# Stick-breaking attention: cumulative products from rounded high and low parts of L

## The reference

```python
z = einsum('bqhd,bkhd->bhqk', q, k) * scale
log_1m = where(mask, log_sigmoid(-z), 0.0)
rest = cumsum(log_1m, axis=3, reverse=True) - log_1m
a = where(mask, exp(log_sigmoid(z) + rest), 0.0)
out = einsum('bhqk,bkhd->bqhd', a, v)
```

## Time and profile before

| | us |
|---|---|
| median of three runs (2595.11 to 2599.73) | 2596.3 |
| the profiled execution | 2597.36 |
| its span | 2595.4 |
| PE busy | 2520.1 (97%) |
| DVE busy | 1105.5 (43%) |
| ACT busy | 851.9 (33%) |
| POOL busy | 918.0 (35%) |

### The profile page before, as it was taken

One profiled execution on the slowest core, in us unless ns is written; L12 is line 12 of the kernel. 1 busy time (PEld: TensorE's weight loads), 2 busy tenths in 40 slices (PEclk: granted clock), 3 DMA queues, 4 the chain that ended last, 5 costly groups with the idle time before them and its releaser, 6 DMA issues.

```text
span 2595.4 us, 40399 instructions
## 1 busy us (share of the span) xinstructions
PE 2520.1 (97%) x16578; PEld 2205.8 (85%) x16578; DVE 1105.5 (43%) x1722; ACT 851.9 (33%) x1257; POOL 918.0 (35%) x382
## 2 busy tenths in 40 slices
PE   7999997999999999999999999999889999999999
PEld 6888887999999998777999999876566888888887
DVE  3883435365352522222562525434456433622222
ACT  3323322332222334544331222443335333422222
POOL 3221123244444441111354444431223454544443
PEclk9999999999999999999999999999999999999999
DMA  4110112132222221110222222321111322322222
GB/s 160 66 66 34 51 49 90 41 107 97 81 95 84 97 98 54 37 46 17 82 97 98 82 96 81 108 74 49 65 60 55 114 101 94 114 97 94 87 95 97
DMA packets 34002, 208.31 MB, mean 80 GB/s; under 512 B 3771, under 2 KB 7125, under 8 KB 9817
## 3 DMA queue, kind: packets, MB, share of 16 engines
q1 hardware_dynamic: 29552, 202.00, 22.0%
q10 hardware_dynamic: 4328, 4.54, 0.6%
HBM read 204.40 MB, written 2.12 MB: 80 GB/s over the span
## 4 chain that ended last, share of the span: by engine, by line
issue 62%; POOL 22%; PE 15%; POOLq 0%; DMA 0%; ACT 0%; ACTq 0%; DVE 0%; DVEq 0%
POOL wl L2397 22%; PE ps L365 13%; PE ps L318 1%; PE ps L302 1%; DMA arena<-in_extra 0%; POOLq L2396 0%; POOLq L2401 0%; DMA scratch<-arena 0%; PE ps L735 0%; ACT Hh L481 0%; ACT arena L486 0%; ACTq L700 0%; ACT wh L403 0%; PE ps L461 0%; ACTq L701 0%
## 5 line engine op out<-in xcount | busy, mean ns | idle before, releaser
L2397 POOL TENSOR_TENSOR wl<-raw,wh 128x1024 fp32r<-128x1024 f32 x376 | 917.7, 2444 | 1660.9 <-ACT wh L403 1660.9
L403 ACT ACTIVATE wh<-raw 128x1024 fp32r<-128x1024 f32 x376 | 395.1, 1054 | 844.2 <-PE ps L365 519.1
L365 PE MATMUL ps<-Hl,wh 128*128 128x264 f32 (+1 forms) x1896 | 489.7, 317 | 0.0
L365 PE MATMUL ps<-Hh,wl 128*128 128x264 f32 (+1 forms) x1896 | 488.0, 316 | 0.0
L365 PE MATMUL ps<-Hh,wh 128*128 128x264 f32 (+1 forms) x1896 | 487.1, 315 | 0.0
L365 PEld LDWEIGHTS ps<-Hh,wh 128*128 128x128 f32 x1896 | 312.3, 188 | 24.2
L365 PEld LDWEIGHTS ps<-Hl,wh 128*128 128x128 f32 x1896 | 311.6, 188 | 23.5
L365 PEld LDWEIGHTS ps<-Hh,wl 128*128 128x128 f32 x1896 | 311.7, 188 | 22.8
L318 PE MATMUL ps<-Hh,wh 128*128 128x264 f32 (+1 forms) x1056 | 287.1, 336 | 7.0 <-DVE arena L337 6.7
L318 PE MATMUL ps<-Hl,wh 128*128 128x264 f32 (+1 forms) x1056 | 261.3, 312 | 0.0
L318 PE MATMUL ps<-Hh,wl 128*128 128x264 f32 (+1 forms) x1056 | 260.9, 311 | 0.0
(11 more groups left out here) (259 smaller groups left out, 2982.0 us busy)
## 6 DMA issues: line engine op xcount, KB each, us to landing
raw<-in_w_all SPq DMA_DIRECT2D x188, 1024.0 KB, 4.7
X<-in_xT SPq DMA_DIRECT2D x4, 528.0 KB, 9.5
arena<-scratch ACTq DMA_DIRECT2D x2, 1024.0 KB
arena<-in_extra ACTq DMA_DIRECT2D x2, 528.0 KB
out<-X SPq DMA_DIRECT2D x1, 1024.0 KB, 4.2
out<-X SPq DMA_DIRECT2D x4, 256.0 KB, 2.0
arena<-in_extra ACTq DMA_DIRECT2D x2, 264.0 KB
cst<-in_consts SPq DMA_DIRECT2D x1, 448.0 KB, 11.3
```

The source lines that it names most:

```text
L365: mm = pe.matmul(ps[:, 2 * j + h + bank, 0:c1 - c0], w[:, j, k, :], x[:, blk, c0:c1], start=(at == 0 and part == 0), stop=(at == len(ks) - ...
L403: act.activation(wh[:, j], raw[:, j // 2, :, P * (j % 2):P * (j % 2) + P], ACT.Copy).then_inc(hi_split, 1)
L2397: pool.tensor_tensor(wl[:, j], raw[:, j // 2, :, P * (j % 2):P * (j % 2) + P], wh[:, j].bitcast(F32), ALU.subtract).then_inc(split_ready[j ...
```

## The change

L is written twice: as Lh, rounded to fp32r, and as Ll, what rounding left (also fp32r). The triangle and the square are rounded copies made once by ACT. `stick_cum` gets a `part`, 0 for the high and 1 for the low, and goes for every key tile over all later tiles itself; the sums of tiles on DVE and their semaphore `l_sums` are gone. PE's round is now: high products of step n-1, half of the fill (two groups), low products, the other half, value product, logits, with no exception for the fourth round. DVE computes max(z, 0) + E into Lh, again in f32 into E, and subtracts the one from the other into Ll (semaphore `l_low`). Because steps 2 and 3 of one pair no longer wait for the sums, the columns of tiles 2 to 4 have two places in L, used in turn (`l_turn`). The tables land at another place in the arena.

```diff
-        def stick_cum(pe, d, m):
+        def stick_cum(pe, d, m, part):
...
-            pe.wait_ge(sig["l_made"].sem, m + 1)
-            if x in (1, 2):
-                pe.wait_ge(sig["l_sums"].sem, 2 * b + x)
+            pe.wait_ge(sig["l_low" if part else "l_made"].sem, m + 1)
             for hh in range(2):
                 for s, c0, c1, at in STEP_PARTS[x]:
                     R = KEYTILE[s][1]
...
-                    mm = add("ntri", s, c0)
-                    for s2 in ((s + 1, s + 2) if x == 0 else (s + 1,)):
-                        if s2 <= 4 and max(c0, P * s2) < c1:
-                            mm = add("nones", s2, max(c0, P * s2))
-            sig["cum"].by(mm)
+                    for s2 in range(s, 5):
+                        lo = max(c0, P * s2)
+                        if lo < c1:
+                            rows, a = KEYTILE[s2][1], L_AT[s2] + l_turn(s2, b) - P * s2
+                            tri = d["ntri_r" if s2 == s else "nones_r"]
+                            mm = pe.matmul(ps[0:R, bank + hh, at + lo - c0:at + c1 - c0], tri[0:rows, 0:R],
+                                           d["L"][part][0:rows, hh, a + lo:a + c1], start=False, stop=True,
+                                           skip_group_check=True)
+            if part:
+                sig["cum"].by(mm)
...
             for n in range(STEPS + 2):
-                late = n % 4 == 3
-                if late:
-                    stick_fill(pe, n)
-                if 0 <= n - 1 < STEPS:
-                    stick_cum(pe, d, n - 1)
-                if not late:
-                    stick_fill(pe, n)
+                for part in range(2):
+                    if 0 <= n - 1 < STEPS:
+                        stick_cum(pe, d, n - 1, part)
+                    stick_fill(pe, n, part)
...
             act.activation(d["ident_r"], ident, ACT.Copy)
+            act.activation(d["ntri_r"], d["ntri"], ACT.Copy)
+            act.activation(d["nones_r"], d["nones"], ACT.Copy)
...
                     if n >= 2:
-                        act.wait_ge(sig["l_made"].sem, n - 1)
+                        act.wait_ge(sig["l_low"].sem, n - 1)
...
-                    sig["l_made"].by(v.scalar_tensor_tensor(
-                        out=L[:, :, STEP_L[x]:STEP_L[x] + w], in0=ps[:, bank:bank + 2, 0:w], scalar=0.0,
-                        in1=d["E"][:, n % 2, :, 0:w], op0=ALU.max, op1=ALU.add))
+                    dve.by(v.scalar_tensor_tensor(out=hi, in0=z, scalar=0.0, in1=e, op0=ALU.max, op1=ALU.add))
+                    dve.last(v)
+                    sig["l_made"].by(v.scalar_tensor_tensor(out=e, in0=z, scalar=0.0, in1=e, op0=ALU.max, op1=ALU.add))
+                    sig["l_made"].last(v)
+                    sig["l_low"].by(v.tensor_tensor(lo, e, hi.bitcast(F32), ALU.subtract))
```

More of the change, by code:

```diff
@@ L237, in program @@
             "g_conv", "g_silu", "prod_hi", "cv_tmp", "cv_hi", "cv_lo", "idx", "idx_relu", "idx_added", "z_made",
[L238 to L245, removed]
+            "z_log", "e_made", "l_made", "mask_ready", "cum", "a_exp", "oT_hi", "oT_lo", "rot_made", "rot_done",
+            "ret_s", "ret_a", "ret_o", "ret_var", "ret_std", "hn_sq", "hn_sum", "hn_std", "hn_done", "v_made",
+            "v_copied", "tb_made", "tb_copied", "tb_lo", "idx_dup", "idx_dup_read", "p_scores", "p_lo", "p_logits",
+            "p_exp", "p_diag", "p_turned", "p_copied", "p_av", "p_hi", "row_log", "row_scan", "bc_made", "bc_copied",
+            "m_w", "m_wd", "m_s", "m_a", "m_o", "m_ss", "m_std", "mg_sum", "mg_hi", "memset_done", "stage_dve",
+            "o_used", "row_done", "gain_both", "rs_first", "rs_mean", "rs_second", "gate_act", "row_bias", "out_gate",
+            "u_made", "u_read", "mo_exp", "m_sq", "e_read", "m_h", "m_hi", "m_y", "m_lo", "ret_center", "ret_t",
+            "ret_sum", "ret_sq", "ret_hi", "ret_y", "ret_lo", "l_low")}
         turn_done = [signal(f"turn_done{q}") for q in range(2)]
@@ L1486, in stick_views @@
             at = cut.at
-            L, E, A = cut(2 * TRI, h=2), cut(4 * 432, a=2, h=2), cut(4 * 432, a=2, h=2)
+            E, A = cut(4 * 432, a=2, h=2), cut(4 * 432, a=2, h=2)
             vT = Cut(at)(8 * T1, b=8)
[L1489 to L1492, removed]
+            cut = Cut(cut.at, arena_r)
+            Lh, Ll = cut(2 * TRI_2, h=2), cut(2 * TRI_2, h=2)
+            mask_r, ident_r, ntri_r, nones_r = cut(288), cut(P), cut(P), cut(P)
+            w = Cut(KB * T1 + at)
+            mask, ntri, nones = w(288), w(P), w(P)
+            return dict(V=V, E=E, A=A, vT=vT, mask=mask, ntri=ntri, nones=nones, L=(Lh, Ll), mask_r=mask_r,
+                        ident_r=ident_r, ntri_r=ntri_r, nones_r=nones_r)
+        TRI_2 = TRI + 432
         PAIRS = 8
@@ L1500, in program, with l_turn @@
         L_AT = [832, 432, 160, 16, 0]
+        def l_turn(s, b):
+            return TRI if s >= 2 and b % 2 else 0
         STEP_MASK = [(0, 288), (160, 288), None, (160, 288)]
@@ L1590, in stick_av, with stick_fill @@
             sig["o_used"].by(mm)
-        def stick_fill(pe, n):
+        def stick_fill(pe, n, part):
             b, x = n // 4, n % 4
             if b + 1 < PAIRS:
-                for k in range(4 * (x % 2), 4 * (x % 2) + 4):
-                    stick_group(pe, 2 * (b + 1) + x // 2, k)
+                k = 4 * (x % 2) + 2 * part
+                stick_group(pe, 2 * (b + 1) + x // 2, k)
+                stick_group(pe, 2 * (b + 1) + x // 2, k + 1)
             elif n < STEPS:
-                for k in range(2 * x, min(2 * x + 2, KB - 1)):
-                    out_group(pe, 0, k)
+                if 2 * x + part < KB - 1:
+                    out_group(pe, 0, 2 * x + part)
             elif n == STEPS:
-                pe.wait_ge(sig["a_exp"].sem, STEPS - 1)
-                for k in range(KB - 1):
+                if part == 0:
+                    pe.wait_ge(sig["a_exp"].sem, STEPS - 1)
+                for k in (range(4, KB - 1) if part else range(4)):
                     out_group(pe, 1, k)
@@ L1689, in stick_dve @@
             d = stick_views()
-            L = d["L"]
             evac_units(v, PLAN["c_v"], T1, d["vT"])
@@ L1695, in stick_dve @@
             for n in range(STEPS + 2):
[L1696 to L1706, removed]
-                if n < STEPS:
-                    x = n % 4
-                    w, bank = STEP_COLS[x], Z_BANK[n % 2]
+                if n < STEPS:
+                    b, x = n // 4, n % 4
+                    w, bank, a = STEP_COLS[x], Z_BANK[n % 2], STEP_L[x]
+                    if x == 0:
+                        a += l_turn(2, b)
+                    z, e = ps[:, bank:bank + 2, 0:w], d["E"][:, n % 2, :, 0:w]
+                    hi, lo = (part[:, :, a:a + w] for part in d["L"])
                     v.wait_ge(sig["z_log"].sem, n + 1)
```

## The result

The changed kernel takes 2641.55 us (median of four runs, 2641.08 to 2649.16), the kernel before 2596.02 (four runs): ratio 1.018, 95% interval 1.0159 to 1.020. It is slower by 45.5 us; the prediction said 2622.2 (+25.9) and a range up to 2634. The profiled executions took 2641.1 and 2597.4 us.

A forecast was written before the change was run, and what follows sets the result against it. TensorE was taken to bound the kernel, busy 97% at 2.4 GHz. Terms 25.0+1.1+0.3-0.9+0.4 gave +25.9 us on the profiled 2597.4, so 2623.3, and 2622.2 for the median; range 2604 to 2634.

The forecast's parts named there:

- The bound: Whole kernel: TensorE busy 97% of the span at 2.4 GHz, so a microsecond of matmul work is one of kernel.
- The products: Cumulative products at L1564's successor: 576 records against 384, 13.27 us per pair against 10.14, 25.0 us more in eight pairs.
- 16x16 product: Step 0's cumulative products: one rounded pass of the 16x16 matmul was priced at 0.125 us.
- the f32 break: Where a matmul's number of rows changes: drain 0.095 us and open weight load 0.107 us, taken to hold for fp32r too.
- Rival 1: 16-row products of steps 0 to 2: loads of rounded matmuls stay hidden through changes of rows; 2586 us, 10%.
- The vector side and the waits: Stick-breaking stage: VectorE's added work hides; waits add 1.1 and 0.3, logits save 0.9, the unit's evacuation adds 0.4 us.
- Rival 2: Stage's 32 steps: waits pile up, ACT late by 0.5 us in each, +16 us, 2638 us; 4%.
- The step that failed: Clock during cumulative products: 24 short matmuls at 1060 to 1064 stay at full clock, taken as evidence against rival 3.
- rival 3: Stick-breaking stage: breaks let the granted clock fall to 1.2 GHz over 20 us, costing as much again; 2642 us, 3%.

The follow-up runs named there:

- after_rows128: Changed kernel, but products with the last key tile (16 keys) take and write 128 rows, so no changes of rows: 2596.7 us, ratio 1.0002.
- before_later: Kernel before, with 20 matmuls issued twice at the end of the second FFN, a delay ahead of the last block: 2603.0 us, ratio 1.0032.
- rounded_sums: Changed kernel with 128 rows for the last key tile and running sums back on VectorE, split into high and low parts: 2582.9 us, ratio 0.9958.

## Why the prediction was wrong

- **The bound** was right: PE is busy 343.6 of the stage's 347.3 us, and a microsecond on it is one of the kernel. The row of slices named for the clock is too coarse for it; the view that shows the upper level in the stage is the earlier trace rows, 1.00.
- **The products** were right: 576 records, parts of 2.25, 1.54, 1.67, 0.72 against 2.37, 1.54, 1.67, 0.69, a pair 2.95 us longer against 3.07 (3.13 in products, less 0.06 in the waits named). The one price that was off is the 16x16 product behind another of 16 rows: rows stay, so its load is hidden although the columns change (2.25 for 2.37). The assumption on which all rested, that fp32r pays the f32 break, is shown by `after_rows128`: the same matmuls without changes of rows, and a pair takes 3.9 us less. Rival 1 is out.
- **The vector side and the waits** were right: +1.4 us measured, and the changed kernel's parts wait for DVE in the first and the last pair as said (1.02 and 0.22 us for 1.1 and 0.3). Rival 2 is out: in the changed kernel one weight load of the stage waited for ACT, 0.4 us, in the kernel before eight did, 3.2 us together.
- **The step that failed** is the one that gave rival 3 three chances in a hundred: "the stretch at 1060 to 1064 has 24 such short matmuls and stays at full clock". It took a stretch of f32 products as evidence for fp32r ones, and put the clock at nothing in the sum. In the f32 stretch the columns' own time is 2.03 of the 4.25 us (1216 columns at four cycles and 2.4 GHz). In fp32r it is 0.51 of the 2.25 us of a part, and the breaks stay as they are. Seven falls came, 27.3 us at the lower level. The 36.4 us that the stage lost are 8 x 2.95 = 23.6 for products, 1.2 for the two waits on VectorE, 0.3 for a longer wait on a DMA, and 11.3 that are left for the clock: six falls at 1.43, and a longer one (6.8 us) in the last pair. That these falls go away with the breaks is shown by `after_rows128`; that the array's low use is what brings the clock down is an argument, since no run changed the one without the other.
- **What no step had**: a longer stage moves what comes after it. The last block has stretches at the lower level in the kernel before already, and how long they last depends on when they come: 17.1 us within the block before, 44.4 after, +11.5 us. (The 20 to 24 and 44 to 51 us in the expectation of `before_later` count a fall that lies ahead of the block.) `before_later` shows it without the change, and the table of first falls in all thirteen profiles. What sets the time of the first fall stays open.
- **Luck.** Rival 3 named 2642 and 2641.55 was measured, but not for its reason alone: the falls cost some 11 us in the stage, not its 20, and the last block, which the rival does not have, gave 11.5. The first stretch, whose code is the same, happened to be 4.0 us shorter.

A rule of the Trainium skill was weighed in the prediction ("TensorE: Matmul & The Clock Gate", Part 3, The mechanism: loads overlap running matmuls only where the row group differs). The runs go against the sentence where the rows are equal: loads were hidden there, 0.11 us from one 16-row load to the next. Where 16 rows followed 128 the load stayed open; with its "only" the sentence does not promise overlap there, and the prediction read more into it. The same page of the Trainium skill, in the section Why this matters for your kernels, names idle gaps between bursts of matmuls as what makes throughput drop in mid-kernel. Here the clock fell with PE busy 17.06 of the 17.12 us ahead of it (1050.00 to 1067.12), behind a run of short products with breaks; no gap of the profile was there to close, though its busy time counts the open loads and drains as busy. In `rounded_sums` the two falls did come behind gaps, of 1.44 and 1.97 us.

## What to carry to other kernels

Price a matmul by the distance from its start to the next start: here one of few columns cost 0.11 us for its load whatever its columns, and a change of the number of rows 0.2 us on top; where the rows to come are zero, take all 128 (42.6 us of the stage here for two lines, some 31 in products and the rest in clock). Going from two f32 passes to one fp32r pass leaves the loads and breaks as they are and shortens only the columns between them, so look at the granted clock in the places that get sparser, in windows of a few us and not in the page's slices. And when a change moves a later block, compare that block by itself before the total is laid to the change.

## What was not expected of the hardware

- The granted clock fell to 1.2 GHz with PE busy all the time, in three to eight of the eight pairs, depending on the execution, at a cost of 1.43 us for a fall of 3.4 us.
- One block of unchanged instructions took 314.2 to 314.5 us in three kernels and 317.5 to 325.9 in the others, and its time went with when its first fall came; 2.4 us of delay in the old kernel made 314.4 into 325.7 in the profiled execution.
- A 16-row load behind a 16-row product was hidden although the number of weight columns went from 128 to 16.
